# An expert with two passes moved from place 2 to place 16, its gate weights swept once for both passes

## What is computed

```python
def moe_ffn(x, norm_ffn, w_router, b_router, w_gu, b_gu, w_down, b_down):
    xn = rms_norm(x, norm_ffn)
    logits = xn @ w_router + b_router            # 32 experts
    top_v, top_e = lax.top_k(logits, TOP_K)      # 4 of them for each token
    gates = jax.nn.softmax(top_v, axis=-1)
    ...
    def expert_block(args):
        tok, e = args
        h = xn[tok] @ w_gu[e] + b_gu[e]          # 1024 -> 2048
        gate = jnp.minimum(h[:, :D_FF], SWIGLU_LIMIT)
        up = jnp.clip(h[:, D_FF:], -SWIGLU_LIMIT, SWIGLU_LIMIT)
        return ((up + 1.0) * gate * jax.nn.sigmoid(SWIGLU_ALPHA * gate)) @ w_down[e] + b_down[e]   # 1024 -> 1024
    ...
    return x + out
```

## Time and profile before

| | us |
|---|---|
| median of three runs | 1353.85 |
| lowest and highest | 1353.54 and 1355.93 |
| the profiled execution | 1346.76 |
| its span | 1344.9 |
| TensorE busy in it | 1243.1 |
| VectorE, ScalarE busy | 349.6, 222.8 |
| share of DMA in the chain that ended last | 48% |
| share of TensorE in it | 47% |

### The profile page before, as it was taken

The page is one execution under the profiler, slowest core; times in us unless marked ns, Lnnn a source line. Parts: engine busy times, 40 slices in busy tenths (PEclk is TensorE's granted clock), DMA queues, the critical chain, the costliest instruction groups (busy, mean ns, idle before and its releaser), DMA issues.

```text
span 1344.9 us, 17326 instructions
## 1 busy us (share of the span) xinstructions
PE 1243.1 (92%) x6716; PEld 580.6 (43%) x6716; DVE 349.6 (26%) x879; ACT 222.8 (17%) x479; POOL 16.5 (1%) x26
## 2 busy tenths in 40 slices
PE   6998999999999999999898898989889898988986
PEld 3556777866533434433333233333333333333323
DVE  1552445414561122122121111212112121211213
ACT  2223134410431111111111011110101111010110
POOL 0000000000200000000000000000000000000000
PEclk9999989999979999999999999999999999999999
DMA  9545751289269689999999999999999999999994
GB/s 339 178 128 169 258 158 48 74 288 332 86 249 404 266 345 429 428 428 428 429 429 428 428 428 429 428 429 429 428 429 428 429 428 429 428 429 429 427 409 158
DMA packets 76077, 462.06 MB, mean 344 GB/s; under 512 B 19218, under 2 KB 34178, under 8 KB 51202
## 3 DMA queue, kind: packets, MB, share of 16 engines
q1 hardware_dynamic: 76034, 461.47, 84.8%
HBM read 458.48 MB, written 5.07 MB: 345 GB/s over the span
## 4 chain that ended last, share of the span: by engine, by line
DMA 48%; PE 47%; DVE 2%; SPq 1%; issue 1%; ACT 1%; DVEq 0%; ACTq 0%
DMA arena<-w_down 47%; PE banks L1169 11%; PE banks L1132 8%; PE banks L1824 5%; PE banks L571 4%; PE banks L521 2%; PE banks L745 2%; PE banks L1269 2%; PE banks L1113 1%; PE banks L621 1%; PE banks L536 1%; PE banks L634 1%; PE banks L1073 1%; PE banks L1839 1%; DMA arena<-x_prompt 1%
## 5 line engine op out<-in xcount | busy, mean ns | idle before, releaser
L1132 PE MATMUL banks<-arena 128*64 128x512 f32 x2112 | 472.1, 596 | 37.7 <-DMA arena<-w_gu 37.7
L1132 PEld LDWEIGHTS banks<-arena 128*64 128x64 f32 x2112 | 147.2, 137 | 333.5 <-issue 251.7
L1169 PE MATMUL banks<-arena 128*64 128x512 f32 x1056 | 237.7, 594 | 17.9 <-DMA arena<-w_down 17.8
L1224 DVE TENSOR_SCALAR arena<-banks 128x512 f32<-128x512 f32 x33 | 22.8, 691 | 507.3 <-PE banks L1132 507.3
L1169 PEld LDWEIGHTS banks<-arena 128*64 128x64 f32 x1056 | 72.8, 136 | 164.6 <-issue 118.3
L1199 ACT ACTIVATE arena<-arena 128x512 f32<-128x512 f32 x33 | 20.8, 630 | 546.8 <-DVE arena L1224 546.8
L1247 DVE TENSOR_TENSOR arena<-banks,arena 128x528 f32<-128x528 f32 x68 | 48.1, 707 | 173.6 <-PE banks L1113 173.6
L1824 PE MATMUL banks<-arena 128*128 128x512 f32 (+1 forms) x192 | 79.8, 574 | 0.0
L1113 PE MATMUL banks<-arena 128*128 128x264 f32 x272 | 65.1, 392 | 2.5 <-ACT arena L1210 1.3
L571 PE MATMUL banks<-arena 128*128 128x264 f32 x256 | 61.2, 393 | 0.5 <-ACT arena L784 0.5
L1113 PEld LDWEIGHTS banks<-arena 128*128 128x128 f32 x272 | 50.0, 189 | 23.7 <-issue 12.2
(11 more groups left out here) (330 smaller groups left out, 893.8 us busy)
## 6 DMA issues: line engine op xcount, KB each, us to landing
arena<-w_gu SPq DMA_DIRECT2D x128, 2048.0 KB, 24.9
arena<-w_down SPq DMA_DIRECT2D x64, 2048.0 KB, 25.2
arena<-w_in SPq DMA_DIRECT2D x9, 2048.0 KB, 11.3
arena<-cache_moba_k SPq DMA_DIRECT2D x16, 256.0 KB, 2.7
arena<-cache_moba_v SPq DMA_DIRECT2D x16, 256.0 KB, 2.7
arena<-w_out SPq DMA_DIRECT2D x2, 2048.0 KB, 11.7
arena<-cmp_w_k SPq DMA_DIRECT2D x1, 2048.0 KB, 8.6
arena<-cmp_w_v SPq DMA_DIRECT2D x1, 2048.0 KB, 15.3
```

The source lines that it names most:

```text
L1132: mm = nc.tensor.matmul(banks[64 * x:64 * x + 64, BG + b, :], xgT[:, c % 4, 64 * (c // 4):64 * (c // 4) + 64], w[:, D * b + 512 * x:D * b ...
L1169: mm = nc.tensor.matmul(banks[64 * x:64 * x + 64, BY, :], aT[:, c, 64 * part:64 * part + 64], w[:, 512 * x:512 * x + 512], start=False, st ...
L1224: nc.vector.tensor_scalar(gate, banks[:, BG, :], LIMIT, None, ALU.min).then_inc(S["clip"], 1)
```

## The change

`TWICE` becomes 16, so that passes 16 and 17 have the same expert, and passes 2 and 3 are two ordinary ones. Around passes 16 and 17 all engine programs are written out:

- TensorE does the down products of pass 15 ahead of the gate products of pass 16, gathers and turns the tokens of both passes (those of pass 17 go to a second buffer, `xgT_twin`), and then runs `gate_up_twice`: for each chunk of weights four products for pass 16 and four for pass 17, the latter into banks `BX` and `BT`. A slot is free when both passes have used it.
- Behind it come the turned product of pass 16, the gather of pass 18, the down products of pass 16, `spread`, the turned rows of 18, the turned product of 17 and the down products of pass 17. Step 18 then has no down products.
- The scatter inside the double sweep uses banks `BS`, `BA`, `BS`, `BA`, since `BX` is taken, with a wait for an addition in two places instead of one.
- SP asks for the gate slots of pass q+1 and the down slots of pass q in a loop over 2 to 15, then for the down slots of pass 16, the gate slots of pass 18 (slot s waits until the double sweep has used it twice), and then goes on with gate slots of q+1 and down slots of q from q = 18.
- ScalarE and VectorE follow the same order: on VectorE the product of pass 16 comes ahead of the clipping of pass 17.

```diff
-TWICE = 2
+TWICE = 16
...
+        def gate_up_twice(pe, q, place, order):
...
+            for c in range(KC):
+                s = expert_slot(c // 2)
+                if c % 2 == 0:
+                    pe.wait_ge(ring_in[s], ring_value(c // 2, place))
...
+                for _, rows, first in both:
+                    for b in range(2):
+                        for x in range(2):
+                            mm = nc.tensor.matmul(banks[64 * x:64 * x + 64, first + b, :], rows[:, c % 4, 64 * (c // 4):64 * (c // 4) + 64],
+                                                  w[:, D * b + 512 * x:D * b + 512 * x + 512], start=False, stop=(c == KC - 1), tile_position=(0, 64 * x))
+                    if c % 2:
+                        mm.then_inc(S["used"] if c < KC - 1 else S["gu"], 1)
+                if c == 1:
+                    pe.wait_ge(S["atkept"], q)
+                    scatter(pe, q // 2 - 1, q, order)
...
-            load_down(sp, sp.value_load(order_i[0:1, 2:3], min_val=0, max_val=NEXP - 1), 2)
-            load_gate_up(sp, sp.value_load(order_i[0:1, 4:5], min_val=0, max_val=NEXP - 1), 4)
-            with sp.Fori(4, NEXP) as place:
-                load_gate_up(sp, placed_expert(sp, place + 1), place + 1)
-                load_down(sp, placed_expert(sp, place), place)
+            with sp.Fori(2, TWICE) as q:
+                load_gate_up(sp, placed_expert(sp, q + 1), q + 1)
+                load_down(sp, placed_expert(sp, q), q)
+            load_down(sp, sp.value_load(order_i[0:1, TWICE:TWICE + 1], min_val=0, max_val=NEXP - 1), TWICE)
+            e = sp.value_load(order_i[0:1, TWICE + 2:TWICE + 3], min_val=0, max_val=NEXP - 1)
+            for s in range(4):
+                if s < 3:
+                    sp.wait_ge(S["used"], 3 * TWICE + 2 * s + 2)
+                else:
+                    sp.wait_ge(S["gu"], TWICE + 2)
+                load_expert_slot(sp, e, s)
+            with sp.Fori(TWICE + 2, NEXP) as q:
+                load_gate_up(sp, placed_expert(sp, q + 1), q + 1)
+                load_down(sp, placed_expert(sp, q), q)
...
-            step(3, 2, 2, 1, 1, 0)
-            step(4, 3, 2, 0)
-            with pe.Fori(2, PAIRS - 1) as k:
+            with pe.Fori(1, TWICE // 2 - 1) as k:
+                step(2 * k + 1, 2 * k + 1, 2 * k, 1, k, k - 1)
+                step(2 * k + 2, 2 * k + 2, 2 * k + 1, 0)
+            step(TWICE - 1, TWICE - 1, TWICE - 2, 1, TWICE // 2 - 1, TWICE // 2 - 2)
+            gather(pe, TWICE + 1)
+            down(pe, TWICE - 1, TWICE - 1, 1)
+            turn_rows(pe, TWICE + 1)
+            gate_up_twice(pe, TWICE, TWICE, TWIN_ORDER)
+            pe.wait_ge(S["added"], 2 * TWICE + 1)
+            turn_product(pe, TWICE)
+            pe.wait_ge(S["clip"], 3 * TWICE + 6)
+            gather(pe, TWICE + 2)
+            down(pe, TWICE, TWICE, 0)
+            spread(pe, TWICE // 2, TWICE + 2)
+            pe.wait_ge(S["stkept"], TWICE + 2)
+            turn_rows(pe, TWICE + 2)
+            turn_product(pe, TWICE + 1)
+            down(pe, TWICE + 1, TWICE, 1)
+            step(TWICE + 2, TWICE + 1, None, 0)
...
```

More of the change, by code:

```diff
@@ L1096, in turn_rows, with scatter_banks, scatter @@
             mm.then_inc(S["xturned"], 1)
[L1098 to L1102, removed]
+        def scatter_banks(c, order):
+            return banks[:, order[c]:order[c] + 2, :]
+        def scatter(pe, pair, passes, order=(BS, BX, BA, BS)):
             pe.wait_ge(S["ykept"], 2 * passes)
@@ L1110, in scatter @@
                     pe.wait_ge(S["added"], 4 * pair + 2)
-                out = scatter_banks(c)
+                if c == 2 and order[2] == order[0]:
+                    pe.wait_ge(S["added"], 4 * pair + 2)
+                if c == 3 and order[3] == order[1]:
+                    pe.wait_ge(S["added"], 4 * pair + 3)
+                out = scatter_banks(c, order)
                 for x in range(2):
@@ L1140, in gate_up @@
                     between(c)
+        def gate_up_twice(pe, q, place, order):
+            for k in (0, 1):
+                pe.wait_ge(S["xtkept"], q + k + 1)
+                pe.wait_ge(S["pick"], q + k + 1)
+            pe.wait_ge(S["clip"], 3 * q)
+            both = ((0, xgT, BG), (1, xgT_twin, BX))
+            for half, _, first in both:
+                for b in range(2):
+                    for x in range(2):
+                        nc.tensor.matmul(banks[64 * x:64 * x + 64, first + b, :], pick[0:SPLIT, 64 * half:64 * half + CAP], bias_parts[0:SPLIT, D * b + 512 * x:D * b + 512 * x + 512],
+                                         start=True, stop=False, tile_position=(0, 64 * x))
+            for c in range(KC):
+                s = expert_slot(c // 2)
+                if c % 2 == 0:
+                    pe.wait_ge(ring_in[s], ring_value(c // 2, place))
+                w = ring[:, s, :].rearrange("p (c n) -> p c n", c=2)[:, c % 2, :]
+                for _, rows, first in both:
+                    for b in range(2):
+                        for x in range(2):
+                            mm = nc.tensor.matmul(banks[64 * x:64 * x + 64, first + b, :], rows[:, c % 4, 64 * (c // 4):64 * (c // 4) + 64],
[5 more added lines that the diff above has]
+                    scatter(pe, q // 2 - 1, q, order)
         def spread(pe, pair, passes):
@@ L1191, in keep_rows, with keep_rowsT @@
             nc.scalar.copy(xg, banks[:, BX, :]).then_inc(S["xkept"], 1)
-        def keep_rowsT(act, q):
+        def keep_rowsT(act, q, rows=xgT):
             act.wait_ge(S["xturned"], q + 1)
-            nc.scalar.copy(xgT.rearrange("p a b -> p (a b)"), banks[:, BT, :]).then_inc(S["xtkept"], 1)
+            nc.scalar.copy(rows.rearrange("p a b -> p (a b)"), banks[:, BT, :]).then_inc(S["xtkept"], 1)
         def sigmoid(act, q):
@@ L1472, in step @@
                 gather(pe, q + 1)
-                down(pe, q - 1, before, 1 - half)
+                if before is not None:
+                    down(pe, q - 1, before, 1 - half)
                 if spread_pair is not None:
@@ L1583, in experts_act @@
             step(2, 0, None)
-            with act.Fori(1, PAIRS - 1) as k:
+            with act.Fori(1, TWICE // 2 - 1) as k:
+                step(2 * k + 1, 1, k)
+                step(2 * k + 2, 0, None)
+            step(TWICE - 1, 1, TWICE // 2 - 1)
+            keep_rows(act, TWICE + 1)
+            keep_out(act, TWICE - 1, 1, None)
+            keep_rowsT(act, TWICE + 1, xgT_twin)
+            sigmoid(act, TWICE)
+            keep_productT(act, TWICE)
+            sigmoid(act, TWICE + 1)
+            keep_rows(act, TWICE + 2)
+            keep_out(act, TWICE, 0, TWICE // 2)
+            keep_rowsT(act, TWICE + 2)
+            keep_productT(act, TWICE + 1)
+            step(TWICE + 2, 0, None)
+            with act.Fori(TWICE // 2 + 1, PAIRS - 1) as k:
                 step(2 * k + 1, 1, k)
@@ L1704, in experts_dve @@
             step(2, 0)
-            with dve.Fori(1, PAIRS - 1) as k:
+            with dve.Fori(1, TWICE // 2 - 1) as k:
+                step(2 * k + 1, 1, k, k - 1)
+                step(2 * k + 2, 0)
+            step(TWICE - 1, 1, TWICE // 2 - 1, TWICE // 2 - 2)
+            dve.wait_ge(S["gathered"], TWICE + 1)
+            select(ranks(TWICE + 1))
+            dve.wait_ge(S["half_down"], TWICE)
+            picked(expert(TWICE + 1), 1)
+            dve.wait_ge(S["gathered"], TWICE + 2)
+            select(ranks(TWICE + 2))
+            add(dve, TWICE // 2 - 1, TWIN_ORDER)
+            clip_product(dve, TWICE)
+            product(dve, TWICE)
+            dve.wait_ge(S["prod"], TWICE + 1)
+            clip_product(dve, TWICE + 1, BX)
+            product(dve, TWICE + 1)
+            select_by_slot(dve, TWICE // 2, slot_of[:, TWICE // 2:TWICE // 2 + 1])
+            dve.wait_ge(S["half_down"], TWICE + 1)
+            picked(expert(TWICE + 2), 0)
+            step(TWICE + 2, 0)
+            with dve.Fori(TWICE // 2 + 1, PAIRS - 1) as k:
                 step(2 * k + 1, 1, k, k - 1)
```

13 lines of the change are left out of this document (8 added, 5 removed).

## The result

The changed kernel takes 1368.53 us (median, 1364.87 to 1373.43) against 1353.69 us for the kernel before in the same comparison. The ratio is 1.0148 with an interval of 1.0112 to 1.0184: slower by 1.5%, about 20 us. Forecast were 1373.5 us, that is 19.6 us more. In microseconds the timed runs leave more room than the ratio does: these two medians, of four runs each, differ by 14.8 us, while the kernel before had medians of 1346.85 and 1346.06 in the comparisons of the experiments (17 and 25 runs), 22 us under 1368.53. One of the ten runs of the experiment with both orders took 4474.85 us and is not in the ratio given there.

The account below looks back on a forecast made before the run. The prediction took TensorE to set the pace first, then the transfers, so their standstill reaches the end: 37.8 + 1.0 - 19.2 = +19.6 us, giving 1366.4 us profiled and 1373.5 median, range 1366 to 1383.

Parts of the forecast that it names:

- The idle that goes: Early passes 2 and 3, 430 to 490 us: transfers' standstill at 291 GB/s disappears, -19.2 us.
- The idle that comes: Around the double sweep at place 16: new standstill of the transfers up to pass 19's first gate slot, +37.8 us.
- t = 0: Start of the forecast's clock at place 16: the moment the last down slot of pass 14 lands.
- The wait ahead of the down products of pass 15: Before the double sweep: TensorE idles 18.0 us because the first down slot stands five slots behind, landing at 24.5.
- The request for pass 19: Behind the sweep: SP can ask for its first gate slot only after 93.7; it lands at 101.5, ending a 21.5 us gap.
- The sum: Whole kernel: 37.8 new standstill plus 1.0 for the clock minus 19.2 early standstill, +19.6 us.
- rival 1: Two sweeps overlap, the ring carries them and no idle comes at place 16: 1334.6 us, faster; chance 0.05.
- rival 2: TensorE still lags 18 us at pass 15, so its wait is gone and effects cancel: +0.6 us; chance 0.04.
- rival 4: Early idle stays because something else, the expert list or early slots, holds the requests: 1392.6 us; chance 0.02.
- The clock: Down product of pass 15 likely starts at low clock after 18 us of idle: 1 us, bounds 0 and 8.
- rival 3: Clock stays low for 16 us over the down product and sweep: +26.6 us, 1380.5; chance 0.10.
- The estimate of 9.8: Behind the sweep: if two free down slots could pass SP's wait, 9.8 us less idle, sum +10.

Follow-up runs that it names:

- both orders: Changed kernel, SP asking for down slots of 15 before gate slots of 16, and of 18 before gate slots of 19: 1343.15 us, ratio 0.9991.
- the second experiment: Changed kernel with SP asking for the two down slots of pass 18 ahead of the gate slots of pass 19: 1356.61 us, ratio 1.0077.
- the sweep at once: Changed kernel, double sweep ahead of down products of 15, scatter moved, SP reordered (down slots of 18 before gate slots of 19): 1343.30 us, ratio 0.9975.
- the move alone: Kernel before with the two-pass expert moved to place 16, passes 16 and 17 as ordinary steps without double sweep: 1337.96 us, ratio 0.9939.

## Why the prediction was right

Its account was that of the transfers' standstill, and it held term by term.

- The idle that goes: 19.2 us from 291 GB/s; after it the same stretch runs at 428.
- The idle that comes, with t = 0 at 830.43. The wait ahead of the down products of pass 15 was put at 18.0 us until t = 24.5; it is 17.5 until 24.5. The sweep was put at 36.1 and starts at 36.5. Slots were to come free at 43.0, 53.6, 60.5 and 67.3; SP asks at 43.7, 54.7, 61.6 and 68.4. The down products of pass 17 were to end at 89.9; the next bias comes at 90.8. The request for pass 19 was put at 93.9 (93.7 and 0.2 of signalling) and is seen at 95.0.
- The sum: 38.8 us were said for place 16, the row from 850 to 930 gives 39.9. The net +19.6 stands against +19.0 in the traces and 1.48% of 1353.7, 20.0 us, in the timed runs. Some luck is in the closeness: the rows give a net of 20.7, of which 1.7 do not show at the end.
- The rivals: with 17.5 us of wait at place 16, 428 GB/s early, and a standstill of 39.9 us, rivals 1, 2 and 4 fall. The idle of TensorE was looked for near 810 to 835 us and stands at 837 to 855; 7.5 us of that shift are the later start.
- The clock: I took 1 us between 0 and 8. It was low for the 17 us from 842 to 859, but most of that lay in the wait, so rival 3 falls as well. These rows are the wait and the stretch with the down products of pass 15:

```profile
844.00:856.00 12.00, 1.09 (x4) 0.48 (x6) 0.00 (x0) 0.00 (x0) 0.00 (x0) 0.50 1.01 429
851.00:868.00 17.00, 11.71 (x50) 4.31 (x52) 0.68 (x4) 1.74 (x3) 0.00 (x0) 0.77 0.77 310
```

  By estimate the second slot lands one transfer of 4.9 us behind the first, at 859.8, and its half would have ended at 863.4; it ended at 864.0. So the clock cost 0.6 us there. The Trainium skill (TensorE: Matmul & The Clock Gate, "The HAM clock gate") has it that an idle engine falls to the throttled clock; the trace agrees, 0.50 in the wait.
- The other rule of the Trainium skill that was weighed (DMA: Bandwidth & Descriptors, "Where the ~2 us actually goes": the issuing sequencer waits, not the DMA engine) is borne out by the second experiment: letting the free down slots past SP's wait gave 7.5 us. The estimate of 9.8 in the prediction left out that the first of these slots comes free only 7.5 us ahead of the gate request, so that the transfers of the gate slots then begin 2.3 us later.

What was wrong is small. The two absolute figures were both off: 1366.4 was said for the profiled execution, which took 1373.43, and the later start of the experts, 7.5 us, makes that up; 1373.5 was said for the median, which is 1368.53. That one took over the 7 us by which three runs of before lay above its profiled execution, and here the profiled execution is the slowest of the four. The difference between the kernels is what the sum foretold. And rival 1, that the ring can carry two sweeps, does hold for other orders: its condition, less than 19.2 us of standstill at place 16, is met by the sweep at once (16.5) and by both orders (15.6).

## What to carry to other kernels

Where a queue of transfers sets the end, count its standstill and nothing else: 39.9 against 19.2 us gave the result to within 2 us, though TensorE's own waits changed too. Ask of each new order what it puts ahead of a wait on the queue: one product pulled ahead of five other slots cost 15 us although the transfers ran all the time, because it delayed every later release. Let no request for a slot that is free stand behind a wait for one that is not; here that was worth 7.5 us. And take apart a change that does two things, for here the move alone was worth -0.6% and the sweep that came with it, in its order, +2%.

## What the runs showed of the hardware

The clock fell both behind idles of TensorE and in stretches in which it was busy all the time. The first two rows are of the kernel before, the third is of the changed one, all ahead of the experts:

```profile
165.00:189.00 24.00, 24.00 (x290) 16.62 (x286) 9.59 (x23) 9.50 (x19) 0.52 (x1) 1.00 0.65 214
190.00:195.00 5.00, 5.00 (x21) 4.04 (x22) 2.97 (x17) 1.56 (x7) 0.00 (x0) 0.50 0.76 214
164.00:181.00 17.00, 17.00 (x119) 11.51 (x117) 5.38 (x13) 3.13 (x5) 0.00 (x0) 0.54 0.33 110
```

Before, 24 us of 24 were busy at the full clock, and yet it then stood at 0.50, that is 1.2 GHz, with TensorE still busy. In the changed kernel it was low for most of 17 us in which TensorE was busy throughout; that stretch set in behind two idles of 1.07 and 1.62 us. Before had the same code, idles of 1.07 and 1.61 us at the same place and no low clock behind them.

The first gate product started between 377.5 and 388.3 us over the nine traces. The mean granted clock from 110 us to there goes with it: 0.96 in the two traces that start at 377.5 and 378.6, 0.95 in the four from 379.3 to 382.0, 0.94 at 382.5, and 0.93 in the two at 386.6 and 388.3. That the clock makes the spread is argued from this, not tested; it would be why single executions of these kernels differ by some 8 us, and it is why the part behind the first gate product is the better measure of a change in the experts.
